# A paged decode step on one core: cached keys scored in four column quarters, value pages laid 32 rows deep, page fetches on one queue

## The chip, the cores and the metric

One core of a Trainium2 chip runs the whole program. The metric is the device time of one execution in microseconds (us), the median of three runs. The names used below: TensorE (PE in the profile; its weight loads are PEld), VectorE (DVE), ScalarE (ACT), GpSimd (POOL) and SyncE (SP), which here only issues DMAs. The profile gives TensorE's granted clock as a share of 2.4 GHz, so 0.50 is 1.2 GHz.

## What is computed

One layer of a hybrid decoder for 256 prompt tokens and for 8 decoding sequences of 4 new tokens each, all in fp32. A projection `h @ w_in` feeds two branches, a gated linear recurrence (HGRN2) and block-sparse attention (MoBA), then come two projections, a merge, an output projection and a SwiGLU feed-forward. The part that matters here is the attention of the decoding sequences over their cached pages. Each has 16 pages of 128 tokens with 8 heads of 64:

```python
k_past = cache_k[l][page_table].reshape(bs, n_pages * PAGE_SIZE, AT_HEADS, AT_DH)   # 8 x 2048 x 8 x 64
v_past = cache_v[l][page_table].reshape(bs, n_pages * PAGE_SIZE, AT_HEADS, AT_DH)
...
gate = jnp.einsum('bhqd,bnhd->bhqn', qh, kmean)        # kmean: mean key of each block of 256
_, sel = lax.top_k(gate, ksel)                         # 3 of 8 past blocks per query and head
p = jax.nn.softmax(jnp.concatenate([s_sel, s_own], axis=-1), axis=-1)
o = jnp.einsum('bhqkl,bhqkld->bhqd', p_sel, v_sel) + jnp.einsum('bhql,bqlhd->bhqd', p_own, v_own)
```

The kernels score every cached key, derive the block gate from sums of scores, and add a large negative number to the blocks that aren't chosen, so all 128 pages of keys and all 128 pages of values (a page is 256 KB, 33.5 MB for each of the two) are read.

## The kernel before, in words

The program is written by engine, each with its own instruction list, and semaphores join them. `ring` is an SBUF buffer of four slots of 128 x 2048 floats (1 MB). Everything large passes through it: blocks of `w_ada` and `w_in`, then 32 units of keys, 32 units of values, then the weights of the later projections. A unit is four pages of one sequence.

**Keys.** For unit u (sequence `b = u // 4`, `j = u % 4`) SP loads three pages and ACT the fourth (`load_pages`, L266; ACT's calls are `keys`, L541). Each page takes a `value_load` of its number from `pgt` and then one DMA of 128 x 512 floats. A slot is free when DVE has turned its unit: `turn_keys` (L922) waits for the landing and for TensorE to have used the unit two before (`KT` has two buffers), transposes 32 x 32 squares from the ring into `KT` (L927), and raises `key_slots`, on which the loads wait. TensorE's `cached_keys` (L1354) then makes 16 accumulating matmuls of `Wq` (128 x 128) against 128 columns of `KT` (L1363). `Wq` is a mostly zero matrix that POOL fills for each sequence (`queries`, L392), two buffers. ACT copies a sequence's scores out (`scores`, L584), DVE takes block sums and maxima (`block_sums`, L937, its L940 and L941).

**Between the key units** runs the prompt recurrence: TensorE's `gram` (L1396, matmuls L1408) stands behind units 8, 10, ... 22. Each level goes from TensorE's `gram` to POOL's `diff` (L410, L419 and L420), ACT's `level_exp` (L589), POOL's `scale_level` (L422, L430) and back to the next `gram`. DVE's `keep` (L943, L951) picks the result.

**Gate and softmax.** After the last unit DVE compares the gates (L1015 to L1020), finds the row maxima and folds them over four partition strips (L1026, L1028). TensorE spreads them (L1515), ACT takes the exponentials (L640), and DVE transposes the probabilities into `Pt` with a 32 x 32 stream transpose (L1044).

**Values.** A value unit before is one and the same page number of four different sequences: `load_values` (L259) puts a page of each of the four into a slot, each again 128 x 512 floats, token on the partition. SP loads two of the four, ACT one (`value_pages`, L621), POOL one (L449). TensorE's `values` (L1367) makes four matmuls of 32 columns into the four column strips of the array, N = 512 (L1377), and raises `value_slots`. So sixteen units finish four sequences at once, and `sample_out` runs twice (DVE L1088, TensorE L1458). Between the value units TensorE has the recurrence's outputs (`hgrn_sample_out`, L1439; `o_sum`, L1455; `sample_states`, L1448) and the prompt's attention (`prompt_step`, L1526). Behind the last unit and `sample_out(1)` the projection with `w_proj_a` begins (`dense`, L1259; L1236 to L1238 are its three matmuls, L485 and L806 split its weights).

Of the kernel before, what the change touches and what calls it, by code (L numbers as in the profile page):

```python
# [24 lines left out]
P = 128  # L25
# [25 lines left out]
WQ = 17 * P  # L51
# [6 lines left out]
def constants():  # L58
# [7 lines left out]
    c["fold"] = (p[:, None] % 32 == p[None, :] % 32).astype(float)  # L66
# [5 lines left out]
    for s in range(4):  # L72
        c[f"spread{s}"] = c["fold"] * (p[:, None] // 32 == s)
# [13 lines left out]
    for r in range(32):  # L87
        for b in range(NSEQ):
            for k in range(r % TS + 1):
                own[r, b, b * TS + k] = 0  # L90
# [5 lines left out]
    c["sumheads"] = ((p[:, None] // 32 == np.arange(16)[None, :] // TS) & (p[:, None] % TS == np.arange(16)[None, :] % TS)).astype(float)  # L96
# [16 lines left out]
def build(nc, inp, out):  # L113
# [47 lines left out]
    sb("w_area", [P, 2, WQ])  # L161
# [19 lines left out]
    Qrep = sb("Qrep", [P, PAIRS, 4, TSA], F32, "a_area")  # L181
    Qbd = sb("Qbd", [P, PAIRS, NSEQ, 32], F32, "hA")
# [4 lines left out]
    Wq = sb("Wq", [P, 2, WQ], F32, "w_area")  # L187
    Pt = sb("Pt", [P, NSEQ, SW // 32, 32], F32, "a_area")
# [12 lines left out]
    om = sb("om", [P, AH, DH], F32, "s_area", 3 * HH * TB)  # L201
# [57 lines left out]
    def load_values(queue, u, j, which, landed, group):  # L259

        for q in which:
            pg = queue.value_load(pgt[0:1, bass.ds(u + (q * NPG + 3 * NPG * group), 1)], min_val=0, max_val=pools["cache_v"].shape[1] - 1)  # L262
# [3 lines left out]
    def load_pages(queue, pool, b, j, which, landed):  # L266

        for q in which:
            pg = queue.value_load(pgt[0:1, bass.ds(b * NPG + (4 * j + q), 1)], min_val=0, max_val=pools[pool].shape[1] - 1)
            queue.dma_start(ring[:, KV_SLOT[j], q * 512:(q + 1) * 512], pools[pool][0, bass.ds(pg, 1), :, :].rearrange("o p n -> p (o n)"))\  # L270
                .then_inc(sem(f"{landed}{j}"), 16)

    block = nc.Block()
    with block:

        @block.sync
        def _(sp):
# [19 lines left out]
            for j in range(4):  # L297
                sp.wait_ge(sem("lo_split"), 2 * (NW - NSLOT + j + 1))
                load_pages(sp, "cache_k", 0, j, range(3), "k_landed")
# [5 lines left out]
            for j in range(4):  # L305
                sp.wait_ge(sem("key_slots"), 4 * NSEQ - 3 + j)
                load_values(sp, j, j, range(2), "v_landed", 0)
# [4 lines left out]
            for group in range(2):  # L312
                with sp.Fori(4 * group + (group == 0), 4 * group + 4) as r:
                    for j in range(4):
                        sp.wait_ge(sem("value_slots"), r * 4 + (j - 3))
                        load_values(sp, r * 4 + j, j, range(2), "v_landed", group)
# [45 lines left out]
        def _(pool):  # L362
# [23 lines left out]
            pool.memset(Wq[:, :, :], 0.0).then_inc(sem("wq_zero"), 1)  # L386
            pool.wait_ge(sem("wq_zero"), 1)
# [4 lines left out]
            def queries(b, levels=0):  # L392


                if b >= 2:
                    pool.wait_ge(sem("kt_used"), 4 * (b - 1))
                for a in range(4):
                    rows = slice(32 * a, 32 * a + 32)
                    step = 2 * P + TS
                    dst = Wq[rows, b % 2, a * 32:a * 32 + AH * step].rearrange("p (h x) -> p h x", x=step)[:, :, 0:2 * P]  # L400
                    if a == 0 and b >= 2:
                        pool.wait_ge(sem("lv_diff"), min(levels + 2, 7))
                        if levels:
                            pool.wait_ge(sem("lv_ready"), levels)
                    ins = pool.tensor_copy(dst.rearrange("p h (c y) -> p h c y", y=P)[:, :, :, 0:TS],
                                           Qrep[rows].rearrange("p a s t -> p (a s) t").rearrange("p (h c) t -> p h c t", c=2)[:, :, :, b * TS:(b + 1) * TS])
                ins.then_inc(sem("wq_ready"), 1)
                pool.wait_ge(sem("wq_ready"), b + 1)
# [25 lines left out]
            queries(0)  # L434
            queries(1)
# [3 lines left out]
            queries(2)  # L439
            pool.wait_ge(sem("kin_ready"), 1)  # L440
            for li in range(7):
                scale_level(li)
                if li + 2 < 7:
                    diff(li + 2)
                if li % 2 == 0:
                    queries(3 + li // 2, li + 1)
            queries(7, 7)

            for j in range(4):  # L449
                pool.wait_ge(sem("key_slots"), 4 * NSEQ - 3 + j)  # L450
                load_values(pool, j, j, [3], "v3_landed", 0)
# [340 lines left out]
        def _(dve):  # L792
# [321 lines left out]
            for h in range(AH):  # L1114
# [4 lines left out]
                if h < HH:  # L1119
                    o_normed(h)  # L1120
# [529 lines left out]
```

## Time and profile before

| what | us |
|---|---|
| median of 3 runs (lowest, highest) | 799.46 (792.03, 802.95) |
| the profiled execution | 801.46 |
| its span, first to last instruction | 799.5 |
| TensorE busy / weight loads busy | 713.2 / 624.9 |
| VectorE busy | 411.5 |
| ScalarE busy | 263.7 |
| GpSimd busy | 87.5 |
| mean granted TensorE clock | 0.933 |
| DMA moved | 168.88 MB, mean 211 GB/s |

The span lies 2.0 us under the profiled execution's own time, and that time 2.0 us over the median. Busy shares are averages over stages that have different limits: up to about 214 us the dense work of `w_ada` and `w_in`, from 217.7 to 364 us the keys, to 378 us gate and softmax, to 483 us the values, then dense work again to the end. The change touches only what lies between 214 and 487 us.

### The profile page before, as it was taken

To read this page: it belongs to the slowest core of one execution; us is meant where nothing else is said; L and a number is where in the kernel's file an instruction comes from. 1 tells how busy PE (TensorE), PEld (TensorE's weight loads), DVE (VectorE), ACT (ScalarE), POOL (GpSimd) and SP (SyncE) were. 2 spreads that over 40 slices of the span, in tenths; PEclk is the share of its full clock that TensorE was granted. 3 is DMA by queue.
4 is the path that set the end of the run, shared out by engine and by line. 5 is a ranking of instruction groups with operands and counts; after the bars stand their busy time and mean duration, and the time that the engine had idled before them with its cause. 6 is when DMAs were issued, how large, how long until landed. Compare 5 with 4: busy or idle time off the path is not lost.

```text
span 799.5 us, 13906 instructions
## 1 busy us (share of the span) xinstructions
PE 713.2 (89%) x5179; PEld 624.9 (78%) x5179; DVE 411.5 (51%) x494; ACT 263.7 (33%) x374; POOL 87.5 (11%) x127
## 2 busy tenths in 40 slices
PE   4669999999898999994997878995599999999995
PEld 1268998999888999993542337994599999999994
DVE  0553224237396777767237735657644535453426
ACT  1244234344461111003021223344354645432422
POOL 2040000010130256100111110000300000000000
PEclk9879999999999999997657998998799999999997
DMA  9866886882577678786859899651155465544301
GB/s 324 302 259 227 317 299 231 317 297 93 177 212 229 206 235 233 236 269 175 314 173 347 281 375 357 220 178 35 52 158 166 151 188 158 177 132 160 130 1 60
DMA packets 94260, 168.88 MB, mean 211 GB/s; under 512 B 6449, under 2 KB 37865, under 8 KB 91010
## 3 DMA queue, kind: packets, MB, share of 16 engines
q1 hardware_dynamic: 76562, 137.68, 50.8%
q10 hardware_dynamic: 14368, 19.86, 8.2%
q0 software_dynamic: 3280, 10.64, 3.5%
q8 instruction: 35, 0.57, 0.3%
q14 instruction: 15, 0.12, 0.1%
HBM read 163.44 MB, written 4.72 MB: 210 GB/s over the span
## 4 chain that ended last, share of the span: by engine, by line
PE 79%; DVE 9%; DMA 6%; SPq 2%; ACT 2%; issue 1%; POOL 0%; ACTq 0%; DVEq 0%
PE ps L1236 17%; PE ps L1237 17%; PE ps L1238 17%; PE ps L1363 14%; DMA ring<-cache_v 3%; PE ps L1247 3%; PE ps L1377 3%; PE ps L1408 2%; DMA ring<-w_in 2%; DMA ring<-w_ada 1%; DVE KT L927 1%; SPq L262 1%; PE ps L1439 1%; PE ps L1291 1%; PE ps L1568 1%
## 5 line engine op out<-in xcount | busy, mean ns | idle before, releaser
L1236 PE MATMUL ps<-h_hi,w_hi 128*128 128x288 f32 x704 | 211.9, 301 | 18.8 <-POOL h_lo L378 18.8
L806 DVE TENSOR_TENSOR w_lo<-ring,w_hi 128x1024 fp32r<-128x1024 f32 (+1 forms) x128 | 152.8, 1222 | 147.4 <-ACT w_hi L485 147.3
L1237 PE MATMUL ps<-h_lo,w_hi 128*128 128x288 f32 x704 | 209.4, 297 | 0.0
L1238 PE MATMUL ps<-h_hi,w_lo 128*128 128x288 f32 x704 | 208.5, 296 | 0.0
L485 ACT ACTIVATE w_hi<-ring 128x1024 fp32r<-128x1024 f32 (+1 forms) x128 | 129.9, 1042 | 163.7 <-PE ps L1238 85.5
L1236 PEld LDWEIGHTS ps<-h_hi,w_hi 128*128 128x128 f32 x704 | 133.6, 190 | 26.4 <-issue 14.1
L1238 PEld LDWEIGHTS ps<-h_hi,w_lo 128*128 128x128 f32 x704 | 134.2, 191 | 0.0
L1237 PEld LDWEIGHTS ps<-h_lo,w_hi 128*128 128x128 f32 x704 | 133.9, 190 | 0.1
L1363 PE MATMUL ps<-KT,Wq 128*128 128x128 f32 x1024 | 121.2, 280 | 7.4 <-DVE KT L927 7.4
L1363 PEld LDWEIGHTS ps<-KT,Wq 128*128 128x128 f32 x1024 | 118.9, 196 | 8.6 <-issue 4.1
L927 DVE STREAM_TRANSPOSE KT<-ring 128x2048 f32<-128x2048 f32 x32 | 73.9, 2308 | 36.6 <-PE ps L1363 36.2
L1377 PE MATMUL ps<-ring,Pt 128*32 128x512 f32 x256 | 40.9, 748 | 15.9 <-DMA ring<-cache_v 9.8
L1236 PE MATMUL ps<-f_hi,w_hi 128*128 128x288 f32 x176 | 52.3, 297 | 0.0
L1237 PE MATMUL ps<-f_lo,w_hi 128*128 128x288 f32 x176 | 51.9, 295 | 0.0
L1238 PE MATMUL ps<-f_hi,w_lo 128*128 128x288 f32 x176 | 51.8, 294 | 0.0
L1247 PE MATMUL ps<-ring,cs 128*32 128x512 f32 x192 | 27.6, 690 | 11.8 <-DMA ring<-w_ada 11.8
L1238 PEld LDWEIGHTS ps<-f_hi,w_lo 128*128 128x128 f32 x176 | 33.1, 188 | 0.0
L1237 PEld LDWEIGHTS ps<-f_lo,w_hi 128*128 128x128 f32 x176 | 33.0, 188 | 0.1
L1377 PEld LDWEIGHTS ps<-ring,Pt 128*32 128x32 f32 x256 | 6.8, 124 | 33.6 <-DMA ring<-cache_v 16.3
L1187 DVE TENSOR_TENSOR fu<-ps,fa 128x576 f32<-128x576 f32 x11 | 8.3, 758 | 48.0 <-PE ps L1238 24.5
L1236 PEld LDWEIGHTS ps<-f_hi,w_hi 128*128 128x128 f32 x176 | 33.0, 187 | 0.1
L263 POOL DMA_DIRECT2D ring<-cache_v x32 | 17.3, 540 | 121.5 <-issue 95.0
(282 smaller groups left out, 818.0 us busy)
## 6 DMA issues: line engine op xcount, KB each, us to landing
ring<-w_ada SPq DMA_DIRECT2D x24, 1024.0 KB, 6.6
ring<-cache_k SPq DMA_DIRECT2D x96, 256.0 KB, 3.5
ring<-w_in SPq DMA_DIRECT2D x22, 1024.0 KB, 10.1
ring<-w_gu SPq DMA_DIRECT2D x44, 512.0 KB, 4.7
ring<-cache_v SPq DMA_DIRECT2D x64, 256.0 KB, 5.4
ring<-w_down SPq DMA_DIRECT2D x10, 1024.0 KB, 5.0
ring<-cache_k ACTq DMA_DIRECT2D x32, 256.0 KB, 3.5
ring<-cache_v POOLq DMA_DIRECT2D x32, 256.0 KB, 5.8
```

Of the source, the lines that this page charges most:

```text
L263: queue.dma_start(ring[:, KV_SLOT[j], q * 512:(q + 1) * 512], pools["cache_v"][0, bass.ds(pg, 1), :, :].rearrange("o p n -> p (o n)"))\
L485: act.activation(w_hi[:, par, k, :], slot4(s)[:, k, :], ACT.Copy).then_inc(sem("hi_split"), 1)
L806: dve.tensor_tensor(w_lo[:, par, k, :], slot4(s)[:, k, :], w_hi[:, par, k, :].bitcast(F32), ALU.subtract).then_inc(sem("lo_split"), 1)
L927: dve.transpose(KT[:, u % 2, :, :], ring[:, KV_SLOT[u % 4], :].rearrange("p (g n) -> p g n", n=512)).then_inc(sem("key_slots"), 1)
L1187: dve.tensor_tensor(fu[:, :, :], ps[:, base + 2:base + 4, 0:T], fa[:, :, :], ALU.mult).then_inc(sem("fu_ready"), 1)
L1236: pe.matmul(dst, h, x_hi, start=first, stop=False)
L1237: pe.matmul(dst, h, x_lo, start=False, stop=False)
L1238: return pe.matmul(dst, l, x_hi, start=False, stop=last)
L1247: ins = pe.matmul(ps[32 * i:32 * i + 32, ADA_BANK[g % 2], :], cs[:, k, :], ring[:, n % NSLOT, i * BC:(i + 1) * BC], start=k == 0, stop=k = ...
L1363: ins = pe.matmul(ps[:, b % 2, j * P:(j + 1) * P], Wq[:, b % 2, c * P:(c + 1) * P], KT[:, u % 2, :, c * 32:(c + 1) * 32], start=c == 0, st ...
L1377: ins = pe.matmul(ps[32 * q:32 * q + 32, g, :], Pt[:, 4 * g + q, i, :], ring[:, KV_SLOT[j], q * 512:(q + 1) * 512], start=i == 0, stop=False)
L1408: ins = pe.matmul(ps[:, 2 + 2 * (gi % 2) + tt, h * P:(h + 1) * P], left[:, h, tt * P:(tt + 1) * P], right[:, h, tt * P:(tt + 1) * P], star ...
```

## The change

Five things change together.

1. **Keys.** A unit's 16 matmuls have 32 columns each instead of 128, and go to four different column strips (one for each pair of heads): `Wk` takes the place of `Wq`. The rows of the scores are now (head, strip, query), where the strip is the group of 128 keys. POOL builds `Wk` for all eight sequences ahead of the keys, with a mask `quarter`.
2. **Page fetches.** SP alone fetches all pages of keys and values. It reads four page numbers with one load, ahead of its wait for the slot. ACT and POOL fetch none.
3. **Value units** are four pages of one sequence. Page q goes to partitions 32q to 32q + 31 of the slot, four rows of 512 floats behind one another on each partition.
4. **Probabilities** are turned by TensorE (five transposes for a sequence, `turn_probs`) and copied by DVE to `Pt` and `Pto`. The row maxima are folded through two transposes on TensorE.
5. **`sample_out`** runs once for each sequence instead of twice.

```diff
-    def load_values(queue, u, j, which, landed, group):
-        for q in which:
-            pg = queue.value_load(pgt[0:1, bass.ds(u + (q * NPG + 3 * NPG * group), 1)], ...)
-            queue.dma_start(ring[:, KV_SLOT[j], q * 512:(q + 1) * 512], pools["cache_v"][0, bass.ds(pg, 1), :, :].rearrange("o p n -> p (o n)"))\
-                .then_inc(sem(f"{landed}{j}"), 16)
+    def page_numbers(b, j):
+        return nc.values_load_multi_w_load_instructions(pgt[0:1, bass.ds(b * NPG + 4 * j, 4)], engines=[mybir.EngineType.SP],
+                                                        min_val=0, max_val=pools["cache_k"].shape[1] - 1)[1]
+    def load_values(queue, pages, j):
+        for q, pg in enumerate(pages):
+            queue.dma_start(ring[32 * q:32 * q + 32, KV_SLOT[j], :].rearrange("y (a n) -> y a n", n=512),
+                            pools["cache_v"][0, bass.ds(pg, 1), :, :].rearrange("o (a y) n -> y (o a) n", y=32)).then_inc(sem(f"v_landed{j}"), 16)
...
             with sp.Fori(1, NSEQ) as b:
                 for j in range(4):
+                    pages = page_numbers(b, j)
                     sp.wait_ge(sem("key_slots"), b * 4 + (j - 3))
-                    load_pages(sp, "cache_k", b, j, range(3), "k_landed")
+                    load_keys(sp, pages, j)
...
-                for c in range(16):
-                    ins = pe.matmul(ps[:, b % 2, j * P:(j + 1) * P], Wq[:, b % 2, c * P:(c + 1) * P], KT[:, u % 2, :, c * 32:(c + 1) * 32],
-                                    start=c == 0, stop=c == 15)
+                for m in range(4):
+                    for a in range(PAIRS):
+                        c = 4 * a + m
+                        ins = pe.matmul(ps[32 * a:32 * a + 32, b % 2, j * P:(j + 1) * P], Wk[:, b, m // 2, 2 * a + m % 2, :], KT[:, u % 2, :, c * 32:(c + 1) * 32],
+                                        start=m == 0, stop=m == 3)
                 ins.then_inc(sem("kt_used"), 1)
...
+                if j == 0:
+                    pe.wait_ge(sem("probs_ready"), b + 1)
+                    if b == 1:
+                        pe.wait_ge(sem("own_ready"), 2)
+                    if b >= 2:
+                        pe.wait_ge(sem("ob_s"), b - 1)
+                pe.wait_ge(sem(f"v_landed{j}"), 64 * (b + 1))
+                for a in range(4):
+                    ins = pe.matmul(ps[32 * a:32 * a + 32, b % 2, :], Pt[:, b, a, j, :], ring[:, KV_SLOT[j], a * 512:(a + 1) * 512],
+                                    start=j == 0, stop=j == 3 and a != b % 4)
                 ins.then_inc(sem("value_slots"), 1)
...
+            def turn_probs(b):
+                pe.wait_ge(sem("s_exp"), b + 1)
+                ...
+                for j in range(4):
+                    pe.transpose(ps[:, 2 + b % 2, j * P:(j + 1) * P], S[:, b, j * P:(j + 1) * P], ident)
+                pe.transpose(ps[0:TSA, 1, (b % 4) * P:(b % 4 + 1) * P], S[:, b, 512:SW], ident).then_inc(sem("probs_turned"), 1)
...
+            for b in range(5):
+                turn_probs(b)
             for b in range(NSEQ):
                 for j in range(4):
                     values(b, j)
+                    if b == 0:
+                        if j < 3:
+                            turn_probs(5 + j)
+                        else:
+                            probs_sum()
...
-                    if (b, j) == (6, 3):
-                        sample_out(0)
-            sample_out(1)
+                    if b and j == 1:
+                        sample_out(b - 1)
+            sample_out(NSEQ - 1)
```

How the instructions stand on SP inside the loop over key units, before; one unit between two waits (ISA rows are register and check instructions):

```order
L269 ISA [waits key_slots]
L269 TENSOR_LOAD pgt
L269 ISA x2
L270 ISA
L270 DMA ring<-cache_k 128x512
L269 ISA
L269 TENSOR_LOAD pgt
L269 ISA x2
L270 ISA
L270 DMA ring<-cache_k 128x512
```

And now (L269 is in `page_numbers`, L275 in `load_keys`):

```order
L269 TENSOR_LOAD pgt
L269 ISA x8
L315 REGISTER_ALU
L275 ISA [waits key_slots]
L275 DMA ring<-cache_k 128x512
L275 ISA
L275 DMA ring<-cache_k 128x512
L275 ISA
L275 DMA ring<-cache_k 128x512
L275 ISA
L275 DMA ring<-cache_k 128x512
```

Before, a page's number was loaded behind the wait and right ahead of its DMA, three times for a unit on SP; now one load and four pairs of checks stand ahead of the wait and four DMAs behind it. On TensorE a key unit with the `gram` behind it, before:

```order
L1363 MATMUL ps<-KT,Wq 128x128 x32
L1408 MATMUL ps<-hx_94 128x128 x8
L1363 MATMUL ps<-KT,Wq 128x128 x32
L1408 MATMUL ps<-hx_95 128x128 x8
L1363 MATMUL ps<-KT,Wq 128x128 x32
```

And now:

```order
L1329 MATMUL ps<-KT,Wk 32x128 x32
L1388 MATMUL ps<-hx_97 128x128 x8
L1329 MATMUL ps<-KT,Wk 32x128 x32
L1388 MATMUL ps<-hx_98 128x128 x8
L1329 MATMUL ps<-KT,Wk 32x128 x32
```

The places are the same, two units (32 matmuls) between two `gram`s; only the shape changes. At the head of the values on TensorE, before:

```order
L1515 MATMUL ps<-stat,const 128x8
L1377 MATMUL ps<-ring,Pt 32x512 x16
L1524 MATMUL ps<-stat,const 128x8
L1436 MATMUL ps<-hAs,hvs 128x32
L1439 MATMUL ps<-hqt,S_102 128x4 x8
```

And now, from the third value unit of the first sequence on:

```order
L1343 MATMUL ps<-ring,Pt 32x512 x4
L1362 MATMUL ps<-const,S 128x128 x4
L1363 MATMUL ps<-const,S 32x128
L1343 MATMUL ps<-ring,Pt 32x512 x4
L1350 MATMUL ps<-vtok,Pto 32x512
L1504 MATMUL ps<-stat,const 128x8
L1416 MATMUL ps<-hAs,hvs 128x32
```

The transposes of the probabilities (L1362, L1363) stand on TensorE now, five sequences' ahead of the first value unit and three between the first ones, and every sequence ends with its own tokens (L1350).

## Rows read from the trace of the kernel before

**Rows 1.** The page: the chain that ended last, by line

```profile
PE ps L1236 17%; PE ps L1237 17%; PE ps L1238 17%; PE ps L1363 14%; DMA ring<-cache_v 3%; PE ps L1247 3%; PE ps L1377 3%; PE ps L1408 2%; DMA ring<-w_in 2%; DMA ring<-w_ada 1%; DVE KT L927 1%; SPq L262 1%; PE ps L1439 1%; PE ps L1291 1%; PE ps L1568 1%
```

**Rows 2.** Windows: busy PE, PEld, DVE, ACT, POOL; PE clock, DMA share, GB/s

```profile
252.00:337.00 85.00, 85.00 (x767) 84.02 (x767) 59.32 (x42) 11.36 (x14) 32.20 (x42) 1.00 0.75 229
378.00:483.00 105.00, 90.27 (x476) 40.05 (x480) 49.27 (x107) 21.91 (x60) 15.06 (x28) 0.77 0.85 296
```

**Rows 3.** The chain in order of time, key stage: start us, us, what

```profile
301.78 7.15 PE ps L1363 x64
308.93 1.79 PE ps L1408 x16
...
338.89 25.03 PE ps L1363 x224
```

**Rows 4.** The chain, matmuls of 32 columns: four strips by turns, and one strip

```profile
61.61 1.85 PE ps L1247 x16
...
214.99 1.91 PE ps L1351 x60
```

**Rows 5.** Timeline, SP's queue from 294.5 to 298 us: three fetches of one unit

```profile
294.60 2.67 SPq L270 DMA_DIRECT2D ring<-cache_k  x3
```

**Rows 6.** Line L269, SP's instructions for page numbers: duration ns min/median/max

```profile
L269 SPq FUSED_REGOPS  x180: 51/152/178, 178.0 to 347.8; - x180
L269 SPq TENSOR_LOAD <-pgt x96: 262/270/1041, 177.5 to 347.5; - x96
```

**Rows 7.** Timeline, DVE from 217 to 264 us: idle before, and its releaser

```profile
225.64 2.31 DVE L927 STREAM_TRANSPOSE KT<-ring 128x2048 f32<-128x2048 f32 x1 [1.81 <-PE ps L1363]
...
245.63 2.29 DVE L927 STREAM_TRANSPOSE KT<-ring 128x2048 f32<-128x2048 f32 x1
```

**Rows 8.** Timeline, 283 to 292 us: the other work around one gram

```profile
283.73 1.16 POOL L419 TENSOR_TENSOR hx<-hb 128x512 f32<-128x512 f32 x1 [3.18 <-PE ps L1408]
284.20 1.28 DVE L951 COPY_PREDICATED hA<-lvl,ps 128x1024 f32<-128x1024 uint8 x1
284.85 1.04 POOL L420 TENSOR_TENSOR hx<-hb 128x512 f32<-128x512 f32 x1
285.85 2.52 POOL L430 TENSOR_TENSOR hx<-hx,proj 128x512 f32<-128x512 f32 x2
```

**Rows 9.** Windows (columns of rows 2) while the load of x_sample goes through

```profile
9.50:10.00 0.50, 0.50 (x4) 0.00 (x0) 0.00 (x0) 0.00 (x0) 0.00 (x0) 1.00 1.02 222
10.00:10.50 0.50, 0.07 (x4) 0.00 (x0) 0.00 (x0) 0.00 (x0) 0.00 (x0) 1.00 1.01 221
10.50:11.00 0.50, 0.00 (x0) 0.00 (x0) 0.00 (x0) 0.00 (x0) 0.00 (x0) 1.00 0.95 270
```

**Rows 10.** Timeline of SP's queue: the issue of the load of x_sample

```profile
2.54 0.46 SPq L284 DMA_DIRECT2D xtok<-x_sample  x1
```

**Rows 11.** DMA issues by line: KB each, us from issue to landing

```profile
xtok<-x_sample SPq DMA_DIRECT2D x1, 128.0 KB, 9.8
```

**Rows 12.** Windows: the loads of state_hgrn, and the last pages and first weights

```profile
368.00:370.00 2.00, 0.48 (x5) 0.29 (x3) 1.86 (x5) 0.00 (x0) 0.00 (x0) 1.00 1.17 294
...
478.00:481.00 3.00, 3.00 (x18) 1.23 (x14) 0.00 (x0) 0.01 (x1) 0.00 (x0) 0.56 1.04 384
```

**Rows 13.** The chain in order of time, gate and value stage

```profile
378.20 4.50 PE ps L1377 x24
...
400.59 3.50 PE ps L1439 x16
404.09 1.87 PE ps L1377 x8
...
469.99 7.71 DMA ring<-cache_v
...
482.81 1.03 PE ps L1382 x8
...
487.28 0.42 PE ps L1236
```

More of the change, by code:

```diff
@@ L86, in constants @@
     own = np.full((P, NSEQ, TSA), NEG)
-    for r in range(32):
+    for r in range(P):
         for b in range(NSEQ):
-            for k in range(r % TS + 1):
-                own[r, b, b * TS + k] = 0
+            if r % 16 // TS == b % 4:
+                for k in range(r % TS + 1):
+                    own[r, b, b * TS + k] = 0
     c["own"] = own.reshape(P, -1)
@@ L311, in _ @@
                 sp.dma_start(S0[:, 2 * g:2 * g + 2], inp["state_hgrn"][0, 2 * g:2 * g + 2].rearrange("b h d e -> d b h e")).then_inc(sem("s0_landed"), 16)
[L312 to L316, printed above, removed]
+            with sp.Fori(1, NSEQ) as b:
+                for j in range(4):
+                    pages = page_numbers(b, j)
+                    sp.wait_ge(sem("value_slots"), b * 4 + (j - 3))
+                    load_values(sp, pages, j)
             n = B0
@@ L390, in _, with queries @@
             pool.dma_start(out["v_sample"][0].rearrange("b t h d -> (b t) (h d)"), vtok[0:TSA, 2, :]).then_inc(sem("v_stored"), 16)
[L392 to L408, printed above, removed]
+            def queries(b):
+                for hl in range(2):
+                    ins = pool.tensor_tensor(Wk[:, b, hl].rearrange("p c (x t) -> p c x t", t=TS),
+                                             over(Qrep[:, hl, :, :, b * TS:(b + 1) * TS].rearrange("p a f t -> p (a f) t"), 2, 8),
+                                             over(over(C("quarter").rearrange("p (l x) -> p l x", l=2)[:, hl], 1, 8), 3, TS), ALU.mult)
+                ins.then_inc(sem("wk_ready"), 1)
             def diff(li):
@@ L433, in _ @@
             pool.wait_ge(sem("q_spread"), 1)
-            queries(0)
-            queries(1)
+            for b in range(NSEQ):
+                queries(b)
             pool.wait_ge(sem("b_ready"), 1)
@@ L1120, in _ @@
                     o_normed(h)
+                if h % 2 == 0:
+                    strips_masked(2 + h // 2)
                 if h == 5:
@@ L1149, in y1_squares @@
                     dve.tensor_tensor(proj[:, 8 + a:8 + e, :], proj[:, a:e, :], proj[:, a:e, :], ALU.mult).then_inc(sem("y1_sq"), 1)
-            sample_out(1)
+            strips_masked(7)
+            sample_out(7)
             lo_b(22)
@@ L1348, in _ @@
             pe.wait_ge(sem("q_blocks"), 1)
-            for b in range(NSEQ):
+            for g in range(2):
                 for a in range(PAIRS):
-                    ins = pe.matmul(ps[0:32, 2, b * TSA:(b + 1) * TSA], Qbd[:, a, b, :], proj[:, AK + a, SAMP], start=a == 0, stop=a == PAIRS - 1)
+                    ins = pe.matmul(ps[:, 2, g * TSA:(g + 1) * TSA], Qbd[:, a, g, :], proj[:, AK + a, SAMP], start=a == 0, stop=a == PAIRS - 1)
             ins.then_inc(sem("own_scored"), 1)
@@ L1379, in values @@
-                ins.then_inc(sem("value_slots"), 1)
-                if i == NPG - 1:
-                    for q in range(4):
-                        ins = pe.matmul(ps[32 * q:32 * q + 32, g, :], Pt[0:32, 4 * g + q, NPG, :], vtok[0:32, 2, :], start=False, stop=True)
-                    ins.then_inc(sem("v_summed"), 1)
+                if j == 0:
[4 more added lines that the diff above has]
+                        pe.wait_ge(sem("ob_s"), b - 1)
```

216 lines of the change are left out of this document (90 added, 126 removed).

## The prediction

> **What bounds the kernel now.** I read the chain of waits first: who sets the end. TensorE holds most of it; the dense lines L1236 to L1238 make half of the span, and the key matmuls L1363 another 14% [rows 1]. The change leaves the dense lines alone, so the question is the time between 214 and 487 us. Next the windows by stage. From 252 to 337 us TensorE is busy all the time, DVE for 59 of 85 us, the DMA engines at 0.75 with 229 GB/s [rows 2]: the keys are bound by TensorE. From 378 to 483 us it is the other way round: TensorE's clock is at 0.77 on average and the DMA engines at 0.85, 296 GB/s [rows 2]. The chain in order of time says the same. In the key stage two units cost 7.15 us of matmuls and the `gram` between them 1.79 us, and the last seven units run 25.03 us back to back, 3.58 us each [rows 3]; at the end of the value stage the chain goes through a page load of 7.71 us [rows 13].
>
> **Keys, TensorE.** 16 matmuls of 128 columns go, 16 of 32 columns in four strips come. Lower bound: when four strips work by turns, 16 matmul instructions of N = 512 take 1.85 us, 0.46 us for a round of four [rows 4]; a unit has 8 such rounds (two passes) at a quarter of the N, so 0.93 us. Upper bound for issue alone: 60 instructions of 32 columns with N = 32 in one strip took 1.91 us, 0.032 us each [rows 4], so 32 take 1.0 us. If strips took no turns at all the unit would stay at 3.58 us. I take 1.1 us, near the first two, since the four strips use the same form; at half clock 2 us. TensorE then has 1.1 + 1.1 + 1.8 = 4 us of work for two units and a `gram`, instead of 8.9.
>
> **Keys, what is late next.** Three candidates for two units. DVE: two transposes of 2.31, a `keep` of 1.28 [rows 7, 8] and in every second pair the block sums of 1.3: 6.6 us at the mean. The recurrence: from the end of a `gram`, `diff` 2.1 us (283.73 to 285.85), `scale_level` 2.52 [rows 8], the next `gram` 1.79: 6.6 us with hand-overs, 8.5 at half clock. SP: one fetch now takes (2.67 - 0.33) / 2 = 1.17 us [rows 5]. Of this a number's load is 0.27, its check 0.15 [rows 6], the issue 0.33, the rest address steps and gaps; spreading the gaps evenly gives, as an estimate, 0.40 for the load, 0.26 for the check, 0.52 for address and issue. A unit now needs one load, four checks and four issues, all on SP: 0.40 + 4 x 0.26 + 4 x 0.52 + 0.07 = 3.6 us, 7.2 us for two units. Before it was three whole fetches, 3.5 us. So the shared load saves what the fourth page costs, and SP becomes the bound of the keys. Bounds: 3.1 us if four numbers load and check in the time of two, 4.7 us if each is a whole fetch; I take 3.6, the count of instructions in the order.
>
> When does that start? DVE's own work up to key unit 6 is unchanged; what goes there is the 1.81 us in which its third transpose waited for TensorE [rows 7], and about 0.5 us of smaller steps ahead of the keys (own-token scores as 8 matmuls instead of 32, a memset gone). Before, the transpose of unit 6 began at 245.63, so it now ends near 245.7, which frees the slot for unit 10. From there each issue follows the one before by 3.6 us: unit 31 begins to be issued at 246 + 21 x 3.6 = 321.6 us, lands near 327, and with a transpose and a TensorE unit the keys end at 331 us against 363.9. That is 33 us earlier, and it is the whole gain.
>
> **Gate and softmax.** Before, 364 to 378.2 us, where the first value matmul stands [rows 13]. The row maximum loses five small DVE steps and gains two transposes with hand-overs, about even. Added: values wait for five sequences' exponentials and for TensorE's transposes, about 1 us. First value unit near 346 us.
>
> **Values.** Here the change adds a cost that its TensorE work doesn't show. Each page now goes to 32 partitions instead of 128. The trace has one such load: `x_sample`, 128 KB to 32 partitions, issued at 2.54 us [rows 10] and landed 9.8 us later [rows 11]. While its packets go through, the whole of the DMA engines, busy at 1.01 to 1.02, move 222 and 221 GB/s, and 270 in the half microsecond in which it runs out [rows 9]. Full loads of 128 partitions move 384 at a share of 1.04 [rows 12]. So a load to a quarter of the partitions seems to keep all 16 engines busy at little over half of the rate. At 222 GB/s a unit of 1.05 MB takes 4.72 us, more than SP's 3.6 and TensorE's 1.9, and the value stage is bound by it from the first unit to the last. Bounds: 4.0 us (262 GB/s, near the run-out's 270) if engines drift apart so that quarters overlap, 5.5 us (half of 384) if rows of 2 KB are doubled whole. I take 4.72, the cleanest row.
>
> The Trainium skill (SBUF — State Buffer, "Door 1: The DMA port swizzle") says it from the other side: partitions 0 to 31 reach 8 of 16 ports, some 218 GB/s, and two concurrent loads at partitions 0 and 64 gain only 6%; the trace's 221 and 222 agree, while the 6% no row here shows. By that rule with its 6% a unit would take 4.54 us and the sum below come out 5.8 us lower.
>
> The sum, at the DMA engines: the four units that prefetch start to flow at 327 us, right behind the keys: 4 x 4.72 = 18.9. Then `state_hgrn`, 2.1 MB at 294 GB/s [rows 12]: 7.1, so 353 us. Slots come free from 346 on, and SP at 3.6 us for a unit keeps the queue filled. TensorE is no obstacle: its heaviest units carry 1.87 of values and 4.1 of other work at half clock [rows 13], eight of them in a row, which four slots of lead absorb. 28 units x 4.72 = 132.2: the last lands at 485.2 us. Behind it 1.9 for its matmuls, 0.6 for the own tokens, and from there as before, 487.28 - 483.84 = 3.4 us [rows 13] plus about 1 because the split of `w_proj_a` waits for a load that is queued behind the last unit. So the dense work starts at 492.1 instead of 487.28: +4.8 us. All that follows is unchanged.
>
> The profiled execution took 801.46 us, of which 799.5 are its span; that gives 806.3 for it, and against the median of the runs, 799.46, about 804 us. Gain and loss are each some 35 us; they cancel.
>
> What gets cheaper without effect: ACT and POOL lose 64 and 32 fetches, but neither bounds a stage. `sample_out` runs eight times instead of twice, beside the page loads; `strips_masked` of DVE stands in the prompt's loop, one in 9.4 us, where it fits.
>
> **Rivals.**
> *A, full rate.* The slow half microseconds have another cause, and quarters of a slot load at 384 GB/s. Then SP paces the values. TensorE's heavy units end at 388 us, and 22 units remain, of which three are loaded: 19 x 3.6 = 68, and 4 to land: 460, so 23 us less than before: 777 us. For it: four pages of a unit lie in four different quarters. Against: they stand in one queue behind one another, and rows 9.
> *B, slower.* Small rows double in full: a packet of 2 KB costs twice its time when two engines meet. Units take 5.5 us: 32 x 0.78 = 25 more than forecast: 829 us. It decides from 5.08 us on, where the total passes 2% over before. For it: the loads of rows 9 had rows of 4 and 8 KB, these have 2 KB. [...]
> *C, the strips don't take turns* at N = 128 with operands in four pieces of 32. A key unit stays at 3.6 us, the keys end at about 355 us, and with the slow value loads the total is 825 to 830 us. For it only that this shape doesn't occur before; against it rows 4.
> *D, half clock in the keys.* `gram` at half clock makes the recurrence's round 8.5 us; seven rounds end 9 us later, DVE catches up behind them at 2.64 us a unit, and about 4 us stay, which the 7 us between 346 and 353 hide. Total 804: no rival to the time, only to the steps.
>
> **How the numbers follow.** Forecast (with D) 0.56, A with its halfway cases 0.22, B 0.16, C 0.06. A measurement of this kernel can tell about 2% from no change, 16 us. The forecast's own range is 790 to 814 (4.3 to 5.0 us a unit). A gives 770 to 783 and is nearly all of faster; a tenth of A, where engines drift apart far, ends within 2%. B and C are slower. Range 777 to 826; what lies outside is the better half of A and the tail of B.
>
> **What would show it.** Right: key units 3.6 us apart with TensorE idle between them and SP's queue without a wait; the keys' end near 331 us; windows of the value stage at 215 to 235 GB/s with a DMA share near 1.0; `v_landed` as the releaser of the value matmuls; a unit each 4.7 us; the dense work from 492 us. Wrong: value windows near 300 GB/s or more (A), near 195 (B), TensorE busy throughout the keys (C), or a key pace of DVE's 2.3 to 3.3 us, which would mean that the shared load of numbers costs SP less than counted.

## The result, and the profile after

| | before | after |
|---|---|---|
| median of runs, us | 801.05 (792.03 to 802.95, 4 runs) | 817.33 (813.66 to 818.61, 4 runs) |
| after / before | | 1.022, 95% interval 1.013 to 1.031 |
| profiled execution's span, us | 799.5 | 816.8 |
| TensorE's granted clock, mean | 0.933 | 0.859 |
| keys end (last key matmul) | 363.9 | 339.0 |
| dense work starts (first matmul with `w_hi` behind the values) | 487.3 | 504.9 |
| from there to the end | 312.2 | 311.9 |

(The kernel before has one run more here than at the time of the forecast.)

The changed kernel is slower, by about 2%; the interval reaches from 1.3 to 3.1%. The forecast was 804 us, 0.6% more than before. The keys end 24.9 us earlier. The stretch from there to the dense work takes 165.9 instead of 123.4 us, 42.5 more, and the dense work has not changed. 42.5 - 24.9 = 17.6, and the spans differ by 17.3.

The page of the changed kernel, the chain that ended last by engine and by line (it answers to rows 1):

```profile
PE 67%; SPq 9%; DMA 9%; DVE 8%; issue 4%; ACT 1%; POOL 0%; ACTq 0%; DVEq 0%
PE ps L1200 17%; PE ps L1202 16%; PE ps L1201 16%; DMA ring<-cache_v 5%; SPq L275 5%; PE ps L1343 3%; SPq L269 3%; PE ps L1211 3%; DVE KT L876 2%; DMA ring<-w_in 2%; PE ps L1419 2%; SPq L281 1%; DMA ring<-w_ada 1%; DMA ring<-cache_k 1%; PE ps L1430 1%
```

The key matmuls, 14% of the chain before, are no longer among its larger parts. SP's queue has come in (L275 issues key pages, L269 loads and tests page numbers), and the transfers of `cache_v` have grown. The page's costliest groups and DMA issues say how much (busy us, mean ns of one | idle time before and its releaser; in the last two lines KB each and the median us from issue to landing):

```profile
L876 DVE STREAM_TRANSPOSE KT<-ring 128x2048 f32<-128x2048 f32 x32 | 73.1, 2295 | 12.2 <-DMA ring<-cache_k 9.9
L1329 PE MATMUL ps<-KT,Wk 128*32 128x128 f32 x1024 | 46.4, 342 | 38.6 <-DVE KT L876 38.6
L1343 PE MATMUL ps<-ring,Pt 128*32 128x512 f32 x256 | 49.8, 876 | 17.2 <-DMA ring<-cache_v 17.1
...
ring<-cache_k SPq DMA_DIRECT2D x128, 256.0 KB, 3.7
ring<-cache_v SPq DMA_DIRECT2D x128, 256.0 KB, 9.7
```

A key unit costs TensorE 46.4 / 32 = 1.45 us instead of 3.58, and TensorE idles 38.6 us in front of them. A key page and a value page are both 256 KB from the same queue; the one to 128 partitions lands after 3.7 us, the one to 32 partitions after 9.7, its time in the queue included. The windows of the changed kernel (columns of rows 2) show the value stage evenly slow:

```profile
332.00:352.00 20.00, 12.39 (x107) 10.09 (x95) 12.44 (x23) 3.66 (x9) 0.00 (x0) 0.59 1.05 216
352.00:359.00 7.00, 5.65 (x30) 2.55 (x31) 4.83 (x12) 3.45 (x9) 0.00 (x0) 0.58 1.11 276
359.00:402.00 43.00, 42.83 (x202) 23.09 (x198) 12.82 (x22) 6.51 (x9) 0.00 (x0) 0.68 1.05 217
402.00:408.00 6.00, 4.36 (x22) 0.84 (x14) 2.71 (x11) 0.99 (x4) 0.00 (x0) 0.81 1.08 246
408.00:496.00 88.00, 73.36 (x300) 30.65 (x300) 36.11 (x84) 12.26 (x41) 0.00 (x0) 0.64 1.06 220
498.00:502.00 4.00, 3.16 (x9) 0.66 (x5) 0.75 (x1) 2.00 (x2) 0.00 (x0) 0.50 1.04 386
```

Read the last two columns together. The DMA engines' share is over 1 everywhere: they never run out of packets. But they move 216 to 220 GB/s while value pages are all that there is, 276 while `state_hgrn` (128 partitions) is among them, and 386 at a share of 1.04 as soon as the first weights (128 partitions) follow at 498 us. For the same bytes the engines are busy 1.8 times as long (1.06 / 220 against 1.04 / 386). Before it was 296 at 0.85 [rows 2]. The chain in order of time, the places that answer to rows 3 and 13:

```profile
328.61 6.02 DMA ring<-cache_k
334.65 2.32 DVE KT L876
337.01 1.98 PE ps L1329 x32
...
482.89 13.97 DMA ring<-cache_v
496.90 1.93 PE ps L1343 x8
498.84 1.85 PE ps L1350 x2
500.71 0.76 DVE om L1031
501.52 1.88 PE ps L1444 x8
503.60 1.14 DVE w_lo L752
504.88 0.58 PE ps L1200
```

The last page is issued at 482.9 and lands 14 us later, behind what stands in the queue ahead of it.

### The profile page after: what moved, and what is told of

Its sections match the earlier page's. It is cut to its first block, busy times and chain, and to the rows that moved or that the text cites. A ratio compares the mean times of both kernels' runs of the same rounds, so it can differ in the third digit from the quotient of the medians.

```text
span 816.8 us, 13602 instructions
## 1 busy us (share of the span) xinstructions
PE 692.7 (85%) x5219; PEld 570.7 (70%) x5219; DVE 415.0 (51%) x508; ACT 262.9 (32%) x374; POOL 68.8 (8%) x77
## 4 chain that ended last, share of the span: by engine, by line
PE 67%; SPq 9%; DMA 9%; DVE 8%; issue 4%; ACT 1%; POOL 0%; ACTq 0%; DVEq 0%
PE ps L1200 17%; PE ps L1202 16%; PE ps L1201 16%; DMA ring<-cache_v 5%; SPq L275 5%; PE ps L1343 3%; SPq L269 3%; PE ps L1211 3%; DVE KT L876 2%; DMA ring<-w_in 2%; PE ps L1419 2%; SPq L281 1%; DMA ring<-w_ada 1%; DMA ring<-cache_k 1%; PE ps L1430 1%
## 5 line engine op out<-in xcount | busy, mean ns | idle before, releaser
L1200 PEld LDWEIGHTS ps<-h_hi,w_hi 128*128 128x128 f32 x704 | 133.8, 190 | 26.0 <-issue 12.7
L1329 PE MATMUL ps<-KT,Wk 128*32 128x128 f32 x1024 | 46.4, 342 | 38.6 <-DVE KT L876 38.6
L1329 PEld LDWEIGHTS ps<-KT,Wk 128*32 128x32 f32 x1024 | 35.4, 137 | 47.4 <-DVE KT L876 31.9
L1343 PE MATMUL ps<-ring,Pt 128*32 128x512 f32 x256 | 49.8, 876 | 17.2 <-DMA ring<-cache_v 17.1
L392 POOL TENSOR_TENSOR h_lo<-h,h_hi 128x288 fp32r<-128x288 f32 x16 | 16.4, 1050 | 292.0 <-ACT h_hi L501 292.0
```

The costliest lines, as they stand in the source:

```text
L392: pool.tensor_tensor(h_lo[:, k, :], h32[:, k, :], h_hi[:, k, :].bitcast(F32), ALU.subtract).then_inc(sem("h_lo"), 1)
L1200: pe.matmul(dst, h, x_hi, start=first, stop=False)
L1329: ins = pe.matmul(ps[32 * a:32 * a + 32, b % 2, j * P:(j + 1) * P], Wk[:, b, m // 2, 2 * a + m % 2, :], KT[:, u % 2, :, c * 32:(c + 1) * 3 ...
L1343: ins = pe.matmul(ps[32 * a:32 * a + 32, b % 2, :], Pt[:, b, a, j, :], ring[:, KV_SLOT[j], a * 512:(a + 1) * 512], start=j == 0, stop=j == ...
```

## The experiments

Ten kernels, each the changed one with the edit shown. GB/s, share (of the DMA engines' time) and "landing" (the median us from a value page's issue to its landing, for SP and POOL where both load) are from the window of 380 to 460 us in the run's profile, a part of the value stage. "Dense from" is the first matmul with `w_hi` behind the values. The ratio is to the runs of the kernel before on the same chip. All but v_rows128 and rows128_no_checks compute what the reference does.

| run | median us | ratio (95%) | GB/s | share | landing | dense from |
|---|---|---|---|---|---|---|
| after | 817.3 | 1.022 (1.013 to 1.031) | 221 | 1.06 | 10.2 | 504.9 |
| v_rows128 | 794.0 | 0.993 (0.990 to 0.997) | 252 | 0.78 | 3.6 | 480 |
| v_stride4 | 817.2 | 1.024 (1.018 to 1.030) | 221 | 0.71 | 3.4 | 503 |
| v_order_0213 | 810.2 | 1.016 (1.010 to 1.021) | 228 | 1.03 | 9.2 | 500 |
| v_two_queues | 812.4 | 1.022 (1.014 to 1.029) | 246 | 1.02 | 9.7, 8.8 | 496 |
| no_id_checks | 811.4 | 1.015 (1.013 to 1.018) | 218 | 1.03 | 12.5 | 493 |
| keys_twice | 821.9 | 1.027 (1.024 to 1.030) | 215 | 1.04 | 11.6 | 512 |
| stride4_no_checks | 781.7 | 0.979 (0.976 to 0.982) | 274 | 0.84 | 3.7 | 467 |
| stride2_no_checks | 811.0 | 1.015 (1.008 to 1.021) | 218 | 1.05 | 11.4 | 495 |
| rows128_no_checks | 774.0 | 0.967 (0.962 to 0.972) | 301 | 0.87 | 4.1 | 465 |
| stride4_pool | 777.6 | 0.974 (0.970 to 0.978) | 314 | 0.91 | 4.6, 5.0 | 458 |

### v_rows128: the same pages on all partitions

```diff
-queue.dma_start(ring[32 * q:32 * q + 32, KV_SLOT[j], :].rearrange("y (a n) -> y a n", n=512), ... "o (a y) n -> y (o a) n", y=32) ...
+queue.dma_start(ring[:, KV_SLOT[j], q * 512:(q + 1) * 512], ... "o p n -> p (o n)") ...
```

> Each value page is loaded as one row of 2 KB on all 128 partitions (as before the change), everything else as in the changed kernel; so keys of a page and probabilities no longer match, and the attention sums of the decoding sequences are left wrong. The same 1.05 MB and the same 512 packets of 2 KB for a unit. Theory (a load to a quarter of the partitions has half of the rate): the value stage leaves 218 GB/s and is over 280 GB/s in its steady part; SP's 3.6 us a unit or TensorE (136 us busy between 345 and 505 us at a clock of 0.65) becomes its bound; the dense work starts at 465 to 480 instead of 504 us, the total is 778 to 793 us. Rival 1 (2 KB packets, or the one queue, are slow whatever their partitions): 218 GB/s stay, total 817. Rival 2 (TensorE's half clock bounds the stage): rate rises only in short stretches, the total stays above 805.

Measured: 794.0, 23 us less than the changed kernel and 1 us above what the theory gave, with 3.6 us to landing. So it is the destination, not the 2 KB packets nor the one queue; rivals 1 and 2 fall. The 252 GB/s of the table mix two stretches. From 380 to 400 us it is 176 GB/s, with TensorE busy all of the 20 us at a granted clock of 0.63; from 400 to 480 us it is 287, which is the rate that the theory wanted in the steady part. So the prediction's "TensorE is no obstacle" holds only behind slow loads. The dense work starts at 480, at the late end of what was expected: from 401 us on the chain goes mostly through SP's queue, whose 3.6 us a unit (3.9 with its branches and late issues) now pace the stage. With all else as changed and only the layout of the value pages set back, the time is a little below that of the kernel before (0.993).

### v_stride4: every fourth partition instead of 32 neighbours

```diff
-queue.dma_start(ring[32 * q:32 * q + 32, KV_SLOT[j], :].rearrange(...)
+queue.dma_start(ring[q:128:4, KV_SLOT[j], :].rearrange(...)
...
-act.activation(S[:, b, 0:512], ps[:, b % 2, :], ACT.Copy)
+act.activation(S[:, b, 0:512].rearrange("p (j y g) -> p j g y", j=4, g=4), ps[:, b % 2, :].rearrange("p (j g y) -> p j g y", j=4, g=4), ACT.Copy)
```

> The same result as the changed kernel, but token y of a strip of page q lies on partition 4y+q instead of 32q+y: each load still has 32 partitions with four rows of 2 KB, now every fourth partition of the 128. ACT writes the score columns in that order, DVE's block sums and `choose` read them with a stride (some 0.1 to 0.5 us more a sequence). Theory (what counts is which partitions, by the ports that they lie on, not how many): the value stage runs as with 128 partitions, over 280 GB/s, total 778 to 795 us. Rival 1 (a load to 32 partitions is slow wherever they are): 218 GB/s, total 817 to 822.

Measured: 817.2, where the theory gave 778 to 795 and over 280 GB/s. By the total the theory has failed and rival 1 is right. The windows say something else. Changed kernel, then this run, both from 380 to 460 us:

```profile
380.00:460.00 80.00, 73.07 (x289) 29.56 (x281) 40.05 (x83) 15.77 (x41) 0.00 (x0) 0.65 1.06 221
```

```profile
380.00:460.00 80.00, 71.63 (x295) 28.36 (x294) 41.66 (x85) 15.88 (x41) 0.00 (x0) 0.69 0.71 221
```

The same 221 GB/s, but at a share of 0.71 instead of 1.06: these DMA engines idle nearly a third of the time. Each load is fast (3.4 us to landing); there are too few. The line that issues them, in the changed kernel and in this run (duration ns min/median/max), says why:

```profile
L281 SPq DMA_DIRECT2D ring<-cache_v x64: 316/317/927, 381.2 to 458.4; - x64
```

```profile
L281 SPq DMA_DIRECT2D ring<-cache_v x65: 602/602/1337, 380.0 to 457.8; - x65
```

SP takes 0.60 us to issue a load to strided partitions, 0.32 us for one to neighbours. Four of them with the number work make 4.65 us a unit, 4.9 on average from 401 to 455 us with branches and late issues, by chance about the 4.8 us that the transfers took before. Who waits confirms the turn: in the changed kernel SP waited for slots, here for nothing in that window. The changed kernel, SP's queue from 380 to 460 us (us in total, times, longest):

```profile
SPq L281 <- PE ps L1343: 21.2, 7, 6.7
```

So one bound had been taken away and another one of the same size put in its place, and the total could not tell. Two later runs, no_id_checks and stride4_no_checks, take work from SP, without the new layout and with it.

### no_id_checks: SP relieved, in keys and values

```diff
-min_val=0, max_val=pools["cache_k"].shape[1] - 1)[1]
+min_val=0, max_val=pools["cache_k"].shape[1] - 1,
+skip_runtime_bounds_check_because="page ids index the pools")[1]
```

> As the changed kernel, but SP loads the four page numbers of a unit without testing them against their bounds: four tests of 0.26 us go from each unit, for keys and values. Same result. Theory (SP's issuing bounds the keys, the rate into 32 partitions the values): SP needs 2.5 to 2.6 us for a key unit, the pace falls from 3.7 to the next limit, DVE with the recurrence at about 3.3, the keys end 8 to 10 us earlier (330 instead of 339), the value stage keeps 4.8 us a unit and 218 GB/s, and the total is 807 to 811. Rival 1 (the recurrence or TensorE's half clock bounds the keys already): they end at 339, total 816 to 818. Rival 2 (SP bounds the values too): value units 3.7 us apart, total below 795.

Measured: 811.4, expected 807 to 811. The intervals of this run and of the changed kernel overlap, so the gain of 6 us is not clear of noise by the totals; the profiles (the profiled execution is 9.1 us shorter) show where it comes from. The last key transpose starts at 325.2 instead of 334.6, and DVE, which had waited 9.9 us for keys, waits 1.0. The transposes in the window from 246 to 340 us and what DVE sat idle for, in the changed kernel:

```profile
L876 DVE STREAM_TRANSPOSE KT<-ring x26: 2257/2302/2312, 243.8 to 334.6; 128x2048 f32<-128x2048 f32 x26
its engine sat idle before it (us, times) until:
  DMA ring<-cache_k: 9.9, 6
  PE ps L1329: 2.3, 1
```

and in no_id_checks:

```profile
L877 DVE STREAM_TRANSPOSE KT<-ring x25: 2255/2289/2312, 244.2 to 325.2; 128x2048 f32<-128x2048 f32 x25
its engine sat idle before it (us, times) until:
  PE ps L1330: 2.5, 2
  DMA ring<-cache_k: 1.0, 1
```

So SP paced the keys; from 246 to 330 us it now waits 15.6 us for slots that DVE frees, where it had waited for nothing. Behind it stands DVE with 70.7 us of work in the 79 from 246 to 325, together with the recurrence: in the chain of 246 to 330 us DVE's transposes have 26%, POOL's steps of the recurrence 18% and TensorE's `gram` 15%. The value stage kept its 218 GB/s with landings of 12.5 us: SP's spare time is no help there; it waits 51.5 us for slots from 345 to 485 us. Both halves of the theory hold, both rivals fall.

### keys_twice: does TensorE have slack in the keys?

```diff
-for m in range(4):
+for m in [0, 1, 2, 3] * 2:
     for a in range(PAIRS):
```

> Each unit's 32 key matmuls are issued twice (the second round of four chunks adds to the first by starting anew, so the scores are the same); all else as in the changed kernel. Theory (TensorE has slack in the keys since strips work side by side): 1.1 us more for a unit at full clock, 2.2 + 0.9 for its share of `gram` = 3.1 us, below SP's 3.6: the keys end within 3 us of 339, total 815 to 822. Rival C of the prediction (strips take no turns, a unit of 3.6 us of TensorE): the keys would be over 7 us a unit and end beyond 420, total over 880. If TensorE stays at half clock: 2 x 2 + 1.8 = 5.8 us a unit and a total up to 870; the clock is then the bound.

Measured: 821.9, 5 us more, with intervals that overlap. The second rounds are 32 x 1.10 = 35 us of TensorE's time; the last key transpose moves by only 2.9 us (334.6 to 337.5), inside the 3 us of the theory. The key matmuls from 217 to 345 us, changed kernel and this run:

```profile
L1329 PE MATMUL ps<-KT,Wk 128*32 128x128 f32 x1024 | 46.4, 342 | 38.6 <-DVE KT L876 38.6
```

```profile
L1329 PE MATMUL ps<-KT,Wk 128*32 128x128 f32 x2048 | 70.7, 298 | 32.2 <-DVE KT L876 32.0
```

A round of a unit takes 70.7 / 64 = 1.10 us, the value that the prediction had taken for full clock; in the changed kernel it is 1.45. From 246 to 337 us TensorE is busy 60.6 of 91 us in the changed kernel, at a granted clock of 0.78; with the second rounds it is busy 72.0 us, at 0.96 (before: all of the time, at 1.00 [rows 2]). Rival C, 3.6 us a unit, is dead: strips work side by side in this shape.

### v_order_0213 and v_two_queues: two halves of the partitions at once

```diff
-for q, pg in enumerate(pages):
+for q, pg in ((0, pages[0]), (2, pages[2]), (1, pages[1]), (3, pages[3])):
```

> SP issues the four pages of a unit in the order 0, 2, 1, 3, so that neighbours in the queue lie in different halves of the partitions (0 to 31, 64 to 95, 32 to 63, 96 to 127). Same loads, same result. Theory (a queue works its loads off one after the other, two halves meet only where one runs out): up to 6% in the value stage, so 0 to 9 us less: 808 to 817. Rival (engines drift apart by whole pages, and it is halves that collide): 260 GB/s or more and 790 to 800 us.

For v_two_queues SP issues `pages[0:2]` of each value unit and POOL, in a loop of its own, the other two.

> POOL's queue fetches the value pages 2 and 3 of each unit (partitions 64 to 127), SP's the pages 0 and 1 (0 to 63), so that loads to both halves are in flight side by side; keys as in the changed kernel. Same result. Theory (each half of the partitions takes about 220 GB/s alone, and the queue order is what keeps one half idle): if two loads in flight help, the value stage reaches 260 to 384 GB/s and the total 778 to 800. Rival (by the 6% that the Trainium skill, SBUF - State Buffer, Door 1: The DMA port swizzle, gives for two concurrent loads at partitions 0 and 64): 231 GB/s, total 808 to 812. If the DMA engines themselves were slow: 817.

Measured, the order: 228 GB/s instead of 221, 3% more, and a median 7 us below the changed kernel's, though the two intervals overlap. That is the theory's size, and its rival (260 GB/s) falls. Two queues: 246 GB/s in the window, and 257, 268 and 251 in the three stretches of 20 us from 420 to 480, so 14 to 21% over 221. That lies between the theory (260 to 384) and its rival (231). By the total (812.4, intervals overlap) little is left of it, in part because the first value pages from POOL's queue now stand among SP's last keys: the last key page takes 12.7 us to land instead of 6.0, and its transpose starts at 342.0 instead of 334.6. So halves help each other somewhat when two queues serve them, and far less than twice. The Trainium skill (SBUF — State Buffer, "Can I just issue two DMAs to hit both halves?") gives 6% for two concurrent loads at partitions 0 and 64; the 3% of one queue lie below that, and the 14 to 21% of two queues above it. Why these two queues reach only 228 to 230 from 380 to 420 us, these runs don't say.

### stride4_no_checks, stride2_no_checks: is it the ports?

stride4_no_checks is v_stride4 without the tests. stride2_no_checks differs from it in where a page lies:

```diff
-ring[q:128:4, KV_SLOT[j], :]
+ring[64 * (q // 2) + q % 2:64 * (q // 2) + 64:2, KV_SLOT[j], :]
```

> Value pages on every fourth partition (as in the run v_stride4) and no tests of the page numbers. In v_stride4 a page load landed 3.4 us after its issue instead of 11.4 and the DMA engines' share was 0.70 instead of 1.06, but SP issued without a pause, 0.60 us for each strided load instead of 0.32, 4.65 us a unit. Theory (the ports bounded the values in the changed kernel, and v_stride4 only put SP in their place at almost the same pace): without 1.04 us of tests a value unit takes 3.6 us, over 280 GB/s, the dense work starts near 475 us instead of 504, and the total is 782 to 792. Rival (the loads stay slow whatever SP does, or TensorE bounds the stage): the total stays at 808 or above, by the keys alone.

> As stride4_no_checks (a strided load of 32 partitions, 0.60 us of SP for each, no tests), but the pages 0 and 1 of a unit lie on the even and the odd ones of partitions 0 to 63, the pages 2 and 3 on those of 64 to 127. Each load is still spread over every second partition, but only within one half of the 128. Same result. Theory (the ports: a half of the partitions has half of them, as the Trainium skill has it under SBUF - State Buffer, Door 1: The DMA port swizzle): a load has half of the rate again, 215 to 225 GB/s at a share near 1.05, total 806 to 813 as in no_id_checks. Rival (neighbouring partitions are what is slow, any spread cures it): 3.6 us a unit, 281 GB/s, total 780 to 786 as in stride4_no_checks.

Measured: 781.7 and 811.0. The second lies inside what the theory gave; the first lies a hair below its 782 to 792, with its dense work at 467 instead of near 475 us and 274 GB/s in the window where over 280 were expected. Both kernels have the same bytes, issues and cost of an issue (0.60 us); besides the layout only the order of the score columns differs, and DVE's strided sums and its two instructions instead of one to mask a sequence. In stride4_no_checks SP is still the bound: from 388 to 456 us the chain runs through its queue, which waits 0.3 us there. From 380 to 460 us, stride4_no_checks and then stride2_no_checks:

```profile
380.00:460.00 80.00, 68.91 (x368) 28.56 (x364) 43.26 (x98) 16.03 (x49) 0.00 (x0) 0.84 0.84 274
```

```profile
380.00:460.00 80.00, 69.72 (x283) 26.06 (x282) 41.97 (x88) 14.34 (x42) 0.00 (x0) 0.69 1.05 218
```

32 partitions that spread over all 128 load at speed, 32 that spread over one half of them load at 218 GB/s, just like 32 neighbours. Between 32 and 128 partitions it is not how many a load has that matters here, nor whether they are neighbours, but which ones. The Trainium skill (SBUF — State Buffer, "Door 1: The DMA port swizzle") has the same border: the partition number's bits 2 to 4 and 6 pick one of 16 ports, from which it follows that 0 to 31 as well as every second one of 0 to 63 reach 8 of them, and every fourth of 128 all 16. The three layouts agree with it. They test bit 6 alone, since each of them has all values of bits 2 to 4; that those count too, no run here shows.

### stride4_pool, rows128_no_checks: what bounds it then

stride4_pool is stride4_no_checks with POOL fetching the fourth value page of each unit; rows128_no_checks is v_rows128 without the tests.

> As stride4_no_checks, and POOL fetches the fourth value page of each unit, so that SP has 0.40 + 3 x 0.78 = 2.75 us for a value unit. Theory: SP no longer bounds the values; the next limit is TensorE in its heavy units (about 6 us each at half clock up to 400 us) and then the 2.75 us of SP and DMA: the stage ends 10 to 20 us earlier than in stride4_no_checks, total 768 to 780. Rival (TensorE's work of 115 to 130 us already fills the stage): no more than 5 us less than stride4_no_checks. With either it should be below the kernel before (799) as well as the changed one (817).

> Value pages as rows of 2 KB on 128 partitions (as in v_rows128, so the attention sums of the decoding sequences are left wrong), and no tests of the page numbers: SP has 2.55 us for a value unit (0.33 an issue). Theory (with ports and SP out of the way the value stage is TensorE's): the dense work starts at 452 to 460 as in stride4_pool, total 770 to 778. Rival (SP was still the bound in stride4_pool with its 2.75 us and POOL's own fetches): below 768.

Measured: 777.6 and 774.0. stride4_pool leaves nothing out and beats both kernels, the one before by 2.6% (2.2 to 3.0) and the changed one by 40 us. It lies 4 us below stride4_no_checks by the medians, with intervals that overlap, and its dense work starts 8.5 us earlier in the profile: less than the 10 to 20 that the theory gave, by the medians the rival's size. rows128_no_checks has the total that its theory gave, and its rival (below 768) falls, but its dense work starts at 465 and not at 452 to 460; its profile is of the slowest of its four executions (779.1). TensorE is busy for most of what is left. stride4_pool from 338 to 458 us, the whole value stage:

```profile
338.00:458.00 120.00, 108.86 (x556) 50.67 (x554) 54.97 (x122) 24.12 (x61) 15.37 (x28) 0.78 0.80 276
```

109 of 120 us, at a granted clock of 0.78. That does not make TensorE the only bound. The chain of this run is TensorE's up to 387 us, with the loads at 138 GB/s from 360 to 380; from 388 to 416 us it goes through small steps of DVE and ACT between TensorE's, and from 422 to 445 us through SP's issues, with the last page 5.6 us behind them. No run takes TensorE's work out, so what the stage would gain by that isn't shown. Part of this work the change had brought: its own-token sums (L1350) and `sample_out` (L1444) run once a sequence, 11.8 and 12.6 us of TensorE in the changed kernel between 345 and 505 us, where the same work of the kernel before took 3.0 and 2.1 (L1382 and L1466, 372 to 487 us). In the changed kernel it is hidden under the transfers. In the chain of stride4_pool it stands with 5 and 4% of these 120 us, 10 us in all, and is a candidate to take out, which was not tried.

## Why the prediction came out as it did

The time was 13 us above the forecast's 804. It lies inside the whole range of 777 to 826, but not inside the forecast's own 790 to 814. The mechanisms held, but for a wait of 1 us at the very end that did not come; three stretches of the sum were too short, all against the change: the last key page landed 7.7 us late, the values took 4.1 us more, the steps behind them 1.1. Together they are the 12.8 us by which the dense work starts later than forecast (504.9 against 492.1). The sign rested on the difference of a gain and a loss of some 35 us each, which the forecast had as +4.8 us and which came out as +17.6: errors of an eighth to a quarter in the two parts make more than a factor of three in the difference.

- **Keys, TensorE: 1.1 us a unit at full clock.** Right: 1.10 in keys_twice, at a mean granted clock of 0.96. The clock did fall (D), to 1.98 us for the last unit.
- **Keys, SP becomes the bound.** Right, shown by no_id_checks, and by SP's queue, which waits for nothing between 246 and 330 us. Its parts were right too: a load of four numbers 0.30, a test with its gap 0.25, an issue with its address 0.52. **But 3.6 us a unit was too small:** unit 10 is issued at 246.4 (forecast 246), unit 31 from 327.05, so (327.05 - 246.4) / 21 = 3.84 us. Missing in the sum were the loop's branch, 0.4 us in every fourth unit, and four issues of 88 that took 0.68 to 1.33 instead of 0.33 us, 2.7 us more together. That is 5 us over 21 units.
- **The last unit lands near 327, keys end 331.** They landed at 334.65 and ended at 339.0: 5 us by the pace, and 2 since the last page took 6.0 us to land and not the few that the sum had given it. The gain of the keys was 24.9, not 33 us.
- **Gate and softmax, first value unit near 346 us.** It stands at 356.0: 8 us by the keys, and 2 since the stretch took 17.0 us instead of 15. This cost nothing, since the DMA engines' share is 1.05 or more throughout.
- **Values, bound by loads into 32 partitions at 222 GB/s.** Right, and the step on which the sign rested. The row of `x_sample`, one small load of half a microsecond, had foretold the rate of 128 page loads within 3%: 216 to 220 GB/s. That it came so close owes something to luck: the two half microseconds of rows 9 moved 0.22 MB and the load has 0.13, so other packets stood among its own. Rival A (full rate) and rival B (half of it, 5.5 us a unit, 191 GB/s) fall by the same windows.
- **The stage's length.** From the last key's landing to the last value's the sum gave 158.2 us; it took 496.9 - 334.65 = 162.3. About 2 of the 4 us are the rate (33.6 MB at 219 instead of 222 GB/s), about 1 is the store `out_state_p` of 0.26 MB, which shares the DMA engines at 402 to 408 us and which the sum had left out; the rest isn't settled.
- **Behind the last value: 6.9 us.** 504.9 - 496.9 = 8.0. The order was as forecast, with the split `w_lo` at its end. But TensorE's steps ran at a granted clock of 0.50 (498 to 502 us): the own tokens took 1.85 us instead of 0.6, the matmuls of `sample_out` 1.88 instead of 1.08. The 1 us put down for a wait of the split did not come.
- **"What gets cheaper without effect", and what costs without effect.** Right while the transfers bound the stage. v_stride4 shows how thin the cover was: SP needed only 0.3 us more for an issue to take the transfers' place.

So the step that was off most is the first number of the value sum, "starts to flow at 327", and behind it the 3.6 us of SP, which measured 3.84. The pieces had been measured correctly, but the pace was added up from its medians alone.

## What to carry to other kernels

Look where a load's destination partitions lie before you look at its bytes: here a GB/s column at little over half of its best with a DMA share above 1 was the sign of a bad destination, and the same GB/s at a share of 0.7 that of a queue that issues too little. When an edit leaves the total unchanged, compare those two columns before you call its theory wrong; here it had swapped one bound for another of the same size. When gain and loss nearly cancel in a forecast, its sign is worth no more than the worse of the two. A change that takes work from the engine that bounds a stage is worth only the distance to the next bound, and a queue's pace has to be counted with its branches and its outliers, not by its median instruction.

## What the runs showed that was not expected

- A load to every fourth or every second partition costs SP 0.60 us to issue, the same load to neighbouring ones 0.32 (128 partitions: 0.33).
- 32 partitions that spread over all 128 took 3.4 to 3.7 us to land for 256 KB, as quickly as 128 of them (3.6 and 4.1).
- Two queues that serve one half of the partitions each reached 251 to 268 GB/s together from 420 to 480 us, 14 to 21% above the 221 of one queue; one queue with the halves in turn only 228.
- With loads that land fast, TensorE and the small steps of DVE and ACT set the pace of a part of the value stage, which the slow loads had hidden: 176 GB/s from 380 to 400 us in v_rows128, 138 from 360 to 380 in stride4_pool.
